# SBUF operands at multiples of 512 bytes, the router's rows by transposes, and matmuls of ones on an idle TensorE

## The chip, the cores and the metric

One core of one Trainium2 chip runs one launch of a hand-scheduled kernel. The metric is the device time of that launch in microseconds. All work is in fp32; products on TensorE are made of two halves of an fp32 number each (below).

## What is computed

The input is 512 tokens of width 1024. Two blocks follow one another.

```python
# first block
h = rglru_block(x, ...)                    # x @ w_in (1024 x 2560), gates, scan over time, @ w_out
x = layer_norm(ALPHA * x + h, ln_g[0, 0], ln_b[0, 0])
f = hier_moe(x, ...)                       # 4 groups x 8 experts, the best group's best 2 experts per token
x = layer_norm(ALPHA * x + f, ln_g[0, 1], ln_b[0, 1])
# second block, for each of two layers
x = x + 0.5 * swiglu(rmsnorm(x), w1_a, w3_a, w2_a)          # 1024 -> 2816 -> 1024
x = x + (gated sum of a Fourier, a convolution and a pooling branch) @ w_o
x = x + 0.5 * swiglu(rmsnorm(x), w1_b, w3_b, w2_b)
```

## The kernel before

**Split products.** Every large matrix product is three fp32r matmuls, of the high and low parts of both operands (`mm3`, lines 596 to 598: `L597` moves the low part of the data past high weights, and so on). ScalarE makes the high part of each 128x1024 block of weights (`w_hi`, `L1074`), VectorE the low part (`w_lo`, `L1699`). A ring of 5 to 14 raw buffers is filled by SyncE's queue, and the splits go into a ring of four. In a matmul one operand is loaded into the array (the stationary one, always 128 columns, 512 bytes per partition) and the other is moved past it: 512 columns in the recurrence, the mixers, the experts and the down products, 256 columns in the up products of the SwiGLUs, which are Strassen-like sums of quarters (`xf_hi`, `xf_lo`, and `e_hi`, `e_lo` for the combinations of weights).

**Stages in order of time** (us from the span's start): the recurrence to 222; layer norm, router and tables to 283; sixteen pairs of experts to 854; their combination to 892; then SwiGLU, mixers, SwiGLU for each of two layers to 2965; the rows of the result.

**The router's stage.** VectorE adds the residual to each 128-token tile of `x_tok` and normalises it (`L1804`, `L1789`, `L1812`). TensorE transposes it (`L602`), ScalarE applies gain and bias on the way to `x1T` (`L1167`), TensorE multiplies with the router's weights (`logits`, `L649`). Meanwhile GpSimd applies gain and bias to the rows in `x_tok` (`L1529`, `L1531`, with `gb` broadcast from HBM) and stores them to HBM (`x_rows`, `L1533`), from where the experts gather them. VectorE then chooses groups and experts in a chain of small steps (`L1844` to `L1866`), TensorE counts ranks (`L677`), VectorE computes places (to `L1916`), TensorE builds the table of token numbers with one-hot operands in fp32 (`L683`), VectorE turns it into indices, GpSimd issues the gathers (`L1542`), and TensorE transposes the gathered rows for the first pair (`x_turn`).

**Where operands lie.** Tensors stand one behind another in each partition, in the order of the `sb(...)` calls; a tensor that opens an `ExitStack` that was closed before begins again where that one began. In the program as built `raw` begins at byte 16,512. From the sizes it follows that, modulo 512 bytes, `raw`, `w_hi` and `w_lo` begin at 128; `x_tok`, `xc`, `x_hi`, `x_lo`, `g_hi`, `xg_hi`, `xf_hi`, `e_hi` and nearly all other matmul operands of the dense stages at 192; `xeT_hi`, `hT_hi`, `xe` and `hd` of the experts at 288. Slices of 128 fp32 columns keep these offsets.

**Queues.** SyncE loads the weights; ScalarE loads `gb` and the router's weights; GpSimd stores `x_rows`, gathers and scatters rows and loads the `sums` of the SwiGLUs. Each engine runs in program order and waits on semaphores.

Of the kernel before, what the change touches and what calls it, by code (L numbers as in the profile page):

```python
# [13 lines left out]
P = 128  # L14
# [58 lines left out]
C_ROW4 = C_SLOT + 2 * TT  # L73
# [136 lines left out]
def bank_table():  # L210
# [18 lines left out]
    for tt in range(TT):  # L229
        for half in range(2):  # L230
            use(("turn", tt, half), "x1t", 8 * tt + 4 * half + 4)
    use("lgt", "lgc", 2)
    use("rank", "lgc", 3)
# [75 lines left out]
xgh xgl xhi xhi2 xin xlo xlo0 xn xn2 xnv xr xtn yea yev yhi ylo yy zf zp zz""".split()  # L309


def build(nc, io):
    with ExitStack() as ctx:
# [12 lines left out]
        bank = [ctx.enter_context(nc.psum_tensor(f"bank{i}", [P, 512], F32)) for i in range(8)]  # L326
        raw = sb("raw", [P, NRAW, W])
# [4 lines left out]
        ones = sb("ones", [P, P])  # L332

        with ExitStack() as first:
# [15 lines left out]
            with ExitStack() as moe:  # L350
                raw_more = sb("raw_more", [P, NMORE, W], into=moe)
                gb = sb("gb", [P, 2, D], into=moe)
# [11 lines left out]
                oneh = sb("oneh", [P, 2 * TT, P], into=moe)  # L364
                blkh = sb("blkh", [P, 2 * TT, NBLK], into=moe)
                tabs = sb("tabs", [P, 4, NBLK], into=moe)
# [4 lines left out]
                cnt = sb("cnt", [P, 1], U32, moe)  # L371
                sil = sb("sil", [P, 2, FE], into=moe)
# [209 lines left out]
        def tensor_program(e):  # L582
# [21 lines left out]

            def in_tile(j):
# [40 lines left out]
            def logits(tt):  # L646
                e.wait_ge(s["x1t"], 8 * tt + 8)
                for k in range(DT):
                    f = e.matmul(bank[7][0:NG + NE, tt * P:(tt + 1) * P], wr[:, k, :], x1T[:, k, tt * P:(tt + 1) * P],  # L649
                                 start=k == 0, stop=k == DT - 1)  # L650
                f.then_inc(s["lgm"], 1)

            e.wait_ge(s["par"], 32)
            e.wait_ge(s["router"], 64)
# [15 lines left out]

            b = free_bank("rank")
# [53 lines left out]

            x_turn(0)
# [66 lines left out]
            def up_pair(i, j):  # L793
# [261 lines left out]
        def scalar_program(e):  # L1055
# [95 lines left out]
            e.dma_start(gb[:, 0, :], io["ln"][0:1, :].partition_broadcast(P)).then_inc(s["router"], 16)  # L1151
            e.dma_start(gb[:, 1, :], io["ln"][1:2, :].partition_broadcast(P)).then_inc(s["router"], 16)
# [3 lines left out]
            for tt in range(TT + 1):  # L1156
# [3 lines left out]
                if tt >= 1:  # L1160
                    a = tt - 1
                    for half in range(2):
                        e.wait_ge(s["turn"], 2 * a + half + 1)
                        b = bank_of(("turn", a, half))
                        for n in range(4):
                            k = 4 * half + n
                            e.activation(x1T[:, k, a * P:(a + 1) * P], b[:, n * P:(n + 1) * P], ACT.Identity,  # L1167
                                         scale=par("ln_g", k), bias=par("ln_b", k)).then_inc(s["x1t"], 1)

# [291 lines left out]
        def pool_program(e):  # L1461
# [62 lines left out]
            for tt in range(TT):  # L1524
                x = x_tok[:, tt, :]
                e.wait_ge(s["turn"], 2 * tt + 2)
                if tt == 0:
                    e.wait_ge(s["router"], 64)
                e.tensor_tensor(x, x, gb[:, 0, :], ALU.mult).then_inc(s["x1g"], 1)  # L1529
                e.wait_ge(s["x1g"], 2 * tt + 1)  # L1530
                e.tensor_tensor(x, x, gb[:, 1, :], ALU.add).then_inc(s["x1g"], 1)  # L1531
                e.wait_ge(s["x1g"], 2 * tt + 2)
                e.dma_start(x1_dram[tt * P:(tt + 1) * P, :], x).then_inc(s["x1d"], 16)  # L1533

# [11 lines left out]
            e.wait_ge(s["lgm"], TT)  # L1546
# [1001 lines left out]
```

## Time and profile before

| | |
|---|---|
| median of 3 runs | 2981.72 us (2980.78 to 2990.56) |
| the profiled execution, its own time | 2979.92 us |
| its span | 2978.1 us |
| mean granted TensorE clock | 0.979 |
| busy: TensorE matmuls, VectorE, ScalarE, GpSimd | 95%, 74%, 50%, 17% |
| HBM traffic | 175 GB/s over the span, 376 GB/s with the experts |

"Busy" of PE is the time in which at least one matmul is in flight; matmuls overlap, so at full occupation the pace is read from start to start, or from their number in a stretch. The granted clock is 1.00 where TensorE had its 2.4 GHz and 0.50 where it had 1.2 GHz.

### The profile page before, as it was taken

The numbers are of one execution on the slowest core, as the hardware profiler recorded it, in microseconds if no ns is written. First come the engines' busy times: TensorE is split into PE (matmuls) and PEld (weight loads), VectorE is DVE, ScalarE is ACT, GpSimd is POOL, SyncE is SP. The second block draws the span as 40 slices with busy tenths as digits, with TensorE's granted clock in tenths as the row PEclk, the third lists the DMA queues.
The fourth block names the chain that finished last, engine by engine and source line by source line (L and its number), as shares of the span: only waits on it lengthen the run. The fifth ranks groups of instructions, "written<-read, shape, count | busy, mean of one in ns | idle before, by whom it ended". The sixth has DMA issues, their size and how long they took to land.

```text
span 2978.1 us, 41904 instructions
## 1 busy us (share of the span) xinstructions
PE 2832.8 (95%) x16046; PEld 2448.9 (82%) x16046; DVE 2190.4 (74%) x2923; ACT 1498.7 (50%) x1998; POOL 491.8 (17%) x501
## 2 busy tenths in 40 slices
PE   8994999999957999999999999989999999989999
PEld 6673788888847999888888999889998888889997
DVE  6636999999978777766458777787676664687766
ACT  6833788888855444433235444454444332354443
POOL 3214011111012111110112111121111111131111
PEclk9996999999988999999999999999999999999999
DMA  5152999999955555232325655364643323256461
GB/s 216 50 181 77 343 378 374 372 373 375 376 188 138 160 156 163 94 102 93 96 95 139 173 142 169 108 169 132 184 133 101 101 92 101 92 138 181 133 184 59
DMA packets 169579, 516.25 MB, mean 173 GB/s; under 512 B 21536, under 2 KB 22048, under 8 KB 169120
## 3 DMA queue, kind: packets, MB, share of 16 engines
q1 hardware_dynamic: 129600, 422.38, 39.7%
q0 software_dynamic: 37568, 79.72, 12.7%
q10 hardware_dynamic: 2208, 11.43, 1.0%
q8 instruction: 130, 2.13, 0.3%
q14 instruction: 73, 0.60, 0.1%
HBM read 509.24 MB, written 12.58 MB: 175 GB/s over the span
## 4 chain that ended last, share of the span: by engine, by line
PE 82%; DVE 7%; issue 4%; ACT 2%; DMA 2%; POOL 2%; SPq 0%; DVEq 0%; ACTq 0%; POOLq 0%
PE bank L598 27%; PE bank L596 27%; PE bank L597 27%; DVE w_lo L1699 2%; ACT w_hi L1074 1%; PE bank L602 1%; DVE ft L2076 0%; DMA raw<-in_rec_in 0%; DMA raw<-in_w_b 0%; DMA raw<-in_w_a 0%; POOL mv L1506 0%; DVE st L1789 0%; POOL w_lo L1471 0%; DMA sums<-in_w_b 0%; DVE tmp L2132 0%
## 5 line engine op out<-in xcount | busy, mean ns | idle before, releaser
L1699 DVE TENSOR_TENSOR w_lo<-raw,w_hi 128x1024 fp32r<-128x1024 f32 (+3 forms) x481 | 593.2, 1251 | 287.8 <-ACT w_hi L1074 281.1
L1074 ACT ACTIVATE w_hi<-raw 128x1024 fp32r<-128x1024 f32 (+1 forms) x491 | 507.7, 1046 | 292.0 <-PE bank L598 284.8
L596 PE MATMUL bank<-xf_hi,w_lo 128*128 128x256 f32 x2112 | 592.3, 280 | 50.9 <-DVE xf_lo L2082 22.8
L598 PE MATMUL bank<-xf_hi,w_hi 128*128 128x256 f32 x2112 | 588.5, 279 | 0.0
L597 PE MATMUL bank<-xf_lo,w_hi 128*128 128x256 f32 x2112 | 588.4, 279 | 0.0
L596 PEld LDWEIGHTS bank<-xf_hi,w_lo 128*128 128x128 f32 x2112 | 401.1, 190 | 57.1 <-issue 24.4
L597 PEld LDWEIGHTS bank<-xf_lo,w_hi 128*128 128x128 f32 x2112 | 401.1, 190 | 2.4 <-issue 1.0
L598 PEld LDWEIGHTS bank<-xf_hi,w_hi 128*128 128x128 f32 x2112 | 400.7, 190 | 0.0
L1699 DVE TENSOR_TENSOR w_lo<-raw_more,w_hi 128x1024 fp32r<-128x1024 f32 x249 | 296.6, 1221 | 49.2 <-ACT w_hi L1074 46.5
L598 PE MATMUL bank<-g_hi,w_hi 128*128 128x512 f32 x832 | 327.5, 394 | 0.0
L597 PE MATMUL bank<-g_lo,w_hi 128*128 128x512 f32 x832 | 325.9, 392 | 0.0
L596 PE MATMUL bank<-g_hi,w_lo 128*128 128x512 f32 x832 | 323.6, 389 | 0.4 <-DVE g_lo L2119 0.4
L1074 ACT ACTIVATE w_hi<-raw_more 128x1024 fp32r<-128x1024 f32 x249 | 260.4, 1059 | 71.9 <-PE bank L598 71.6
L596 PE MATMUL bank<-xg_hi,w_lo 128*128 128x512 f32 x704 | 277.8, 395 | 0.2 <-issue 0.2
L598 PE MATMUL bank<-xg_hi,w_hi 128*128 128x512 f32 x704 | 277.8, 395 | 0.0
L597 PE MATMUL bank<-xg_lo,w_hi 128*128 128x512 f32 x704 | 277.2, 394 | 0.0
L596 PE MATMUL bank<-w_hi,xeT_lo 128*128 128x512 f32 x512 | 205.4, 401 | 1.5 <-DVE xeT_lo L1952 1.5
L598 PE MATMUL bank<-w_hi,xeT_hi 128*128 128x512 f32 x512 | 205.3, 401 | 0.0
L597 PE MATMUL bank<-w_lo,xeT_hi 128*128 128x512 f32 x512 | 203.3, 397 | 0.0
L597 PEld LDWEIGHTS bank<-g_lo,w_hi 128*128 128x128 f32 x832 | 156.2, 188 | 34.6
L596 PEld LDWEIGHTS bank<-g_hi,w_lo 128*128 128x128 f32 x832 | 156.2, 188 | 34.3 <-DVE g_lo L2119 1.2
L598 PEld LDWEIGHTS bank<-g_hi,w_hi 128*128 128x128 f32 x832 | 156.4, 188 | 31.7
(347 smaller groups left out, 5209.2 us busy)
## 6 DMA issues: line engine op xcount, KB each, us to landing
raw_more<-in_moe SPq DMA_DIRECT2D x249, 512.0 KB, 6.3
raw<-in_moe SPq DMA_DIRECT2D x135, 512.0 KB, 6.3
raw<-in_w_a SPq DMA_DIRECT2D x77, 512.0 KB, 5.0
raw<-in_w_b SPq DMA_DIRECT2D x76, 512.0 KB, 5.2
raw<-in_w_in SPq DMA_DIRECT2D x73, 512.0 KB, 3.6
sums<-in_w_a POOLq DMA_DIRECT2D x88, 256.0 KB, 4.7
sums<-in_w_b POOLq DMA_DIRECT2D x88, 256.0 KB, 4.8
raw<-in_w_a SPq DMA_DIRECT2D x68, 256.0 KB, 6.7
```

Source lines behind the costliest of these rows:

```text
L596: e.matmul(out, a_lo, b_hi, start=start, stop=False, skip_group_check=partial)
L597: e.matmul(out, a_hi, b_lo, start=False, stop=False, skip_group_check=partial)
L598: return e.matmul(out, a_hi, b_hi, start=False, stop=stop, skip_group_check=partial)
L602: last = e.transpose(out[:, n * P:(n + 1) * P], src(n), ident)
L1074: e.activation(split_of(k)[0], source_of(k), ACT.Copy).then_inc(s["hi"], 1)
L1699: e.tensor_tensor(lo, source_of(k), hi.bitcast(F32), ALU.subtract).then_inc(s["lo"], 1)
```

## The change

It has four parts. (1) Unused tensors (`pad_...`) move what stands behind them. In the program as built the weights, `x_hi`, `x_lo`, `xc`, `bd`, `g_hi`, `xg_hi`, `e_hi`, `sums`, `xe`, `hd`, `hT_hi` and `xeT_hi` now begin at 0 modulo 512; `xf_hi` and `xf_lo` begin at 64. (2) The rows of `x_tok` with gain and bias come from transposing `x1T` back on TensorE and copying them with ScalarE, which also issues the stores; GpSimd's eight multiplications and additions and `gb` are gone, and its `memset` of `xe` waits for the last of these transposes. The last half tile of `x1T` is made by VectorE. (3) The token numbers are split into a multiple of 32 and a rest, so that the table is made of bf16 operands. (4) `spin(n)` multiplies `ones` by `ones` n times into bank 7: 14 times at the start, 24 before the table, 16 behind it, and 10 before each of the last three k steps of the first product of the first SwiGLU pair.

```diff
+        sb("pad_raw", [P, 96])
         raw = sb("raw", [P, NRAW, W])
...
         ones = sb("ones", [P, P])
+        sb("pad_ones", [P, 104])
...
-                gb = sb("gb", [P, 2, D], into=moe)
...
-                oneh = sb("oneh", [P, 2 * TT, P], into=moe)
+                oneh = sb("oneh", [P, 2 * TT, P], BF16, moe)
+                numb = sb("numb", [P, 2, 2 * TT, NBLK], BF16, moe)
...
+                sb("pad_router", [P, 112], into=moe)
                 sil = sb("sil", [P, 2, FE], into=moe)
...
+            sb("pad_xf", [P, 16], into=ffn)
             xf_hi = sb("xf_hi", [P, KH, 7 * HALF], F32R, ffn)
             xf_lo = sb("xf_lo", [P, KH, 7 * HALF], F32R, ffn)
+            sb("pad_sums", [P, 112], into=ffn)
...
+            def spin(n):
+                for _ in range(n):
+                    e.matmul(bank[7][:, 0:P], ones[:, :], ones[:, :], start=True, stop=True)
...
+            e.wait_ge(s["cleared"], 2)
+            spin(14)
             for j in range(2 * RT):
...
+            for tt in range(TT):
+                for half in range(2):
+                    b = free_bank(("back", tt, half))
+                    transpose4(lambda n: x1T[:, 4 * half + n, tt * P:(tt + 1) * P], b).then_inc(s["turn"], 1)
             b = free_bank("rank")
...
+            spin(24)
             b = free_bank("table")
             e.wait_ge(s["idx"], 2)
             for n in range(2 * TT):
-                f = e.matmul(b[:, 0:NBLK], oneh[:, n, :], blkh[:, n, :], start=n == 0, stop=n == 2 * TT - 1)
+                e.matmul(b[:, 0:NBLK], oneh[:, n, :], numb[:, 0, n, :], start=n == 0, stop=False)
+                f = e.matmul(b[:, 0:NBLK], oneh[:, n, :], numb[:, 1, n, :], start=False, stop=n == 2 * TT - 1)
...
+            spin(16)
             x_turn(0)
...
                         for k in ks:
+                            if i == 0 and k >= 1:
+                                spin(10)
                             e.wait_ge(s["xgl"], ready + 4 * k + 1)
...
# ScalarE
+            for tt in range(TT):
+                for half in range(2):
+                    e.wait_ge(s["turn"], 2 * TT + 2 * tt + half + 1)
+                    e.activation(x_tok[:, tt, half * T:(half + 1) * T], bank_of(("back", tt, half))[:, :], ACT.Copy) \
+                        .then_inc(s["x1g"], 1)
+                e.wait_ge(s["x1g"], 2 * tt + 2)
+                e.dma_start(x1_dram[tt * P:(tt + 1) * P, :], x_tok[:, tt, :]).then_inc(s["x1d"], 16)
...
# GpSimd
-                e.tensor_tensor(x, x, gb[:, 0, :], ALU.mult).then_inc(s["x1g"], 1)
-                e.tensor_tensor(x, x, gb[:, 1, :], ALU.add).then_inc(s["x1g"], 1)
-                e.dma_start(x1_dram[tt * P:(tt + 1) * P, :], x).then_inc(s["x1d"], 16)
-            e.wait_ge(s["lgm"], TT)
+            e.wait_ge(s["turn"], 4 * TT)
             e.memset(xe[:, :, :], 0.0).then_inc(s["rows"], 1)
...
# VectorE
+            for n in range(4):
+                f = e.tensor_scalar(x1T[:, 4 + n, (TT - 1) * P:], bank_of(("turn", TT - 1, 1))[:, n * P:(n + 1) * P],
+                                    par("ln_g", 4 + n), par("ln_b", 4 + n), ALU.mult, ALU.add)
```

On TensorE, from the transposition of the logits to the first gathered rows, the program before has these rows (`consts` holds the identity):

```order
L649 MATMUL bank<-x1T,wr 36x128 x16
L667 MATMUL bank<-consts,lgT 128x36 x4
L677 MATMUL bank<-chosen,upper_b 128x32
...
L677 MATMUL bank<-chosen,ones_b 128x32 x4
L683 MATMUL bank<-blkh,oneh 128x31 x8
L602 MATMUL bank<-consts,xe 128x128 x8
```

and the changed program these:

```order
L669 MATMUL bank<-x1T,wr 36x128 x16
L687 MATMUL bank<-consts,lgT 128x36 x4
L612 MATMUL bank<-consts,x1T 128x128 x32
L702 MATMUL bank<-chosen,upper_b 128x32
...
L702 MATMUL bank<-chosen,ones_b 128x32 x4
L618 MATMUL bank<-ones 128x128 x24
L709 MATMUL bank<-numb,oneh 128x31
L710 MATMUL bank<-numb,oneh 128x31
...
L618 MATMUL bank<-ones 128x128 x16
L612 MATMUL bank<-consts,xe 128x128 x8
```

The 32 transposes back stand before the ranks, 24 products of ones stand before the table and 16 behind it. The table has 16 products of bf16 in place of 8 of fp32.

On GpSimd the program before has these rows between the recurrence and the first gathers (the first three repeat four times):

```order
L1529 TENSOR_TENSOR x_tok<-x_tok,gb 128x1024
L1531 TENSOR_TENSOR x_tok<-x_tok,gb 128x1024
L1533 DMA x_rows<-x_tok 128x1024
L1547 MEMSET xe 128x3072
L1542 DMA xe<-x_rows,gidx 128x1024 x2
```

and the changed program only these:

```order
L1572 MEMSET xe 128x3072
L1567 DMA xe<-x_rows,gidx 128x1024 x2
```

The eight wide operations and the four stores have left GpSimd; ScalarE has eight copies of 128x512 and the four stores in their place.

## Rows read from the trace of the kernel before

**Rows 1.** The page: the chain that ended last, by engine.

```profile
PE 82%; DVE 7%; issue 4%; ACT 2%; DMA 2%; POOL 2%; SPq 0%; DVEq 0%; ACTq 0%; POOLq 0%
```

**Rows 2.** Waits of TensorE in the whole span: us in total, times, longest.

```profile
PE bank L677 <- DVE chosen L1866: 10.1, 1, 10.1
PE bank L602 <- DMA xe<-x_rows,gidx: 6.7, 1, 6.7
```

**Rows 3.** Busy time by stretch: length, five engines, clock, DMA share, GB/s.

```profile
222.00:283.00 61.00, 23.34 (x147) 19.54 (x146) 46.05 (x107) 14.71 (x40) 28.95 (x18) 0.67 0.18 65
400.00:800.00 400.00, 400.00 (x1790) 323.71 (x1789) 373.79 (x355) 327.76 (x356) 40.24 (x21) 1.00 0.99 376
1345.00:1460.00 115.00, 115.00 (x494) 93.17 (x493) 67.96 (x87) 35.75 (x46) 12.54 (x15) 1.00 0.30 94
```

**Rows 4.** TensorE's groups by form: count, busy us, mean ns, idle before.

```profile
L598 PE MATMUL bank<-xf_hi,w_hi 128*128 128x256 f32 x2112 | 588.5, 279 | 0.0
L598 PE MATMUL bank<-g_hi,w_hi 128*128 128x512 f32 x832 | 327.5, 394 | 0.0
L598 PE MATMUL bank<-xg_hi,w_hi 128*128 128x512 f32 x704 | 277.8, 395 | 0.0
L598 PE MATMUL bank<-w_hi,xeT_hi 128*128 128x512 f32 x512 | 205.3, 401 | 0.0
L598 PE MATMUL bank<-xf_hi,e_hi 128*128 128x256 f32 x352 | 99.6, 283 | 0.0
```

**Rows 5.** TensorE in order of time, one SwiGLU pair: start us, duration.

```profile
1093.18 0.39 PE L596 MATMUL bank<-g_hi,w_lo 128*128 128x512 f32 x1
...
1104.17 0.28 PE L596 MATMUL bank<-xf_hi,w_lo 128*128 128x256 f32 x1
...
1117.77 0.28 PE L596 MATMUL bank<-xf_hi,e_lo 128*128 128x256 f32 x1
...
1120.65 0.28 PE L596 MATMUL bank<-xf_hi,w_lo 128*128 128x256 f32 x1
...
1123.37 0.39 PE L596 MATMUL bank<-g_hi,w_lo 128*128 128x512 f32 x1
```

**Rows 6.** All engines in order of time, router's stage.

```profile
227.92 0.81 DVE L1812 TENSOR_SCALAR x_tok<-x_tok,st 128x1024 f32<-128x1024 f32 x1
...
236.44 3.22 DVE L1812 TENSOR_SCALAR x_tok<-x_tok,st 128x1024 f32<-128x1024 f32 x1
...
244.93 2.90 ACT L1167 ACTIVATE x1T<-bank,params 128x128 f32<-128x128 f32 x8 [1.24 <-PE bank L602]
...
250.93 2.34 POOL L1531 TENSOR_TENSOR x_tok<-x_tok,gb 128x1024 f32<-128x1024 f32 x1
...
251.67 1.63 DVE L1845 TENSOR_TENSOR rt<-lg,sm 128x16 f32<-128x16 f32 x1
...
253.96 2.91 DVE L1849 TENSOR_SCALAR rt<-rt 128x16 f32<-128x16 f32 x1
254.16 2.68 POOL L1547 MEMSET xe<- 128x3072 f32 x1
...
272.24 3.59 PE L683 MATMUL bank<-blkh,oneh 128*128 128x31 f32 x16 [10.47 <-DVE blkh L1916]
```

**Rows 7.** The same view of TensorE: at the start, and where the experts begin.

```profile
8.33 0.76 PE L596 MATMUL bank<-x_hi,w_lo 128*128 128x512 f32 x1 [8.33 <-DVE x_lo L1727]
...
11.32 0.39 PE L597 MATMUL bank<-x_lo,w_hi 128*128 128x512 f32 x1
...
285.94 0.76 PE L596 MATMUL bank<-w_hi,xeT_lo 128*128 128x512 f32 x1 [1.50 <-DVE xeT_lo L1952]
...
291.13 0.40 PE L596 MATMUL bank<-w_hi,xeT_lo 128*128 128x512 f32 x1
```

**Rows 8.** Waits of TensorE from 860 to 975 us, round the first SwiGLU pair.

```profile
PE bank L596 <- DVE xf_lo L2082: 12.2, 2, 6.4
PE bank L596 <- ACT snap L1339: 2.7, 1, 2.7
```

More of the change, by code:

```diff
@@ L72 @@
 C_SLOT = C_EROW + TT * NE
-C_ROW4 = C_SLOT + 2 * TT
+C_REST = C_SLOT + 2 * TT
+C_ROW4 = C_REST + 2 * TT
 C_EDGE = C_ROW4 + 1
@@ L230, in bank_table @@
         for half in range(2):
-            use(("turn", tt, half), "x1t", 8 * tt + 4 * half + 4)
+            use(("turn", tt, half), *(("x1t", 8 * tt + 4 * half + 4) if (tt, half) != (TT - 1, 1) else ("x1v", 1)))
     use("lgt", "lgc", 2)
+    for tt in range(TT):
+        for half in range(2):
+            use(("back", tt, half), "x1g", 2 * tt + half + 1)
     use("rank", "lgc", 3)
@@ L646, in logits @@
             def logits(tt):
-                e.wait_ge(s["x1t"], 8 * tt + 8)
+                if tt < TT - 1:
+                    e.wait_ge(s["x1t"], 8 * tt + 8)
                 for k in range(DT):
+                    if tt == TT - 1 and k % 4 == 0:
+                        e.wait_ge(*((s["x1v"], 1) if k else (s["x1t"], 8 * tt + 4)))
                     f = e.matmul(bank[7][0:NG + NE, tt * P:(tt + 1) * P], wr[:, k, :], x1T[:, k, tt * P:(tt + 1) * P],
@@ L653, in tensor_program @@
             e.wait_ge(s["par"], 32)
-            e.wait_ge(s["router"], 64)
+            e.wait_ge(s["router"], 32)
             for tt in range(TT):
@@ L1161, in scalar_program @@
                     a = tt - 1
-                    for half in range(2):
+                    for half in range(2 if a < TT - 1 else 1):
                         e.wait_ge(s["turn"], 2 * a + half + 1)
@@ L1168, in scalar_program @@
                                          scale=par("ln_g", k), bias=par("ln_b", k)).then_inc(s["x1t"], 1)
+            for tt in range(TT):
+                for half in range(2):
+                    e.wait_ge(s["turn"], 2 * TT + 2 * tt + half + 1)
[3 more added lines that the diff above has]
+                e.dma_start(x1_dram[tt * P:(tt + 1) * P, :], x_tok[:, tt, :]).then_inc(s["x1d"], 16)
             e.wait_ge(s["gat"], 1)
@@ L1522, in pool_program @@
                 weights(2 * RT + k)
[L1524 to L1528, printed above, removed]
-                e.tensor_tensor(x, x, gb[:, 0, :], ALU.mult).then_inc(s["x1g"], 1)
-                e.wait_ge(s["x1g"], 2 * tt + 1)
-                e.tensor_tensor(x, x, gb[:, 1, :], ALU.add).then_inc(s["x1g"], 1)
-                e.wait_ge(s["x1g"], 2 * tt + 2)
-                e.dma_start(x1_dram[tt * P:(tt + 1) * P, :], x).then_inc(s["x1d"], 16)
             def gather(n):
@@ L1816, in vector_program @@
             e.tensor_copy(upper_b[:, :], upper)
+            e.wait_ge(s["turn"], 2 * TT)
+            for n in range(4):
+                f = e.tensor_scalar(x1T[:, 4 + n, (TT - 1) * P:], bank_of(("turn", TT - 1, 1))[:, n * P:(n + 1) * P],
+                                    par("ln_g", 4 + n), par("ln_b", 4 + n), ALU.mult, ALU.add)
+            f.then_inc(s["x1v"], 1)
             e.wait_ge(s["lgm"], TT)
-            e.wait_ge(s["router"], 64)
+            e.wait_ge(s["router"], 32)
             e.tensor_scalar(lgT[:, :], bank[7][0:NG + NE, :], br[:, :], None, ALU.add).then_inc(s["lgc"], 1)
@@ L2506, in lay_out @@
         for tt in range(TT):
-            c[:, C_SLOT + k * TT + tt] = k * T + tt * P + np.arange(P) + 1
+            number = k * T + tt * P + np.arange(P) + 1
+            c[:, C_SLOT + k * TT + tt] = number - number % 32
+            c[:, C_REST + k * TT + tt] = number % 32
     c[:, C_ROW4] = 4 * np.arange(P)
```

12 lines of the change are left out of this document (6 added, 6 removed).

## Prediction

> **What bounds the kernel now.** I read the page first. Matmuls are in flight for 95% of the span, as the table of the profile says, and the chain that ended last runs through TensorE for 82% of it [rows 1]. So I asked next, stretch by stretch, whether TensorE waits or is only slow. With the experts (400 to 800 us) it is busy for all of 400 us, and no release of another engine stands in front of it; VectorE is busy for 373.8 of the 400 us, and the DMA engines for 0.99 of the time at 376 GB/s [rows 3]. In the mixers TensorE is again at 100%, with VectorE at 68 of 115 us [rows 3]. The waits that are left lie in the router's stage, where TensorE works 23 of 61 us at a mean clock of 0.67 [rows 3], waits 10.47 us for the table's operands [rows 6] and 6.7 us for the gathered rows [rows 2], and round the first SwiGLU pair [rows 8].
>
> So two quantities decide: how long the router's chain takes, and at what pace matmuls follow each other where nothing waits. The pace is to be read from start to start, as the durations of rows 4 overlap. One SwiGLU pair gives three paces in a row [rows 5]. The 120 matmuls of 256 columns with a block of `w` as the stationary operand take from 1104.17 to 1117.77, 113.3 ns each. The 24 with `e` take from 1117.77 to 1120.65, 120.0 ns each, and the 24 with `w` behind them 2.72 us, 113.3 ns each. The columns, the clock and the moving tensor (`xf`, at 192 modulo 512) are the same; what differs is the stationary operand, which lies at 128 (64 bytes apart from `xf`, modulo 128) or at 192 (0 apart). The 48 matmuls of 512 columns before them take from 1093.18 to 1104.17, 229.0 ns each; from 1345 to 1460 us of the mixers 494 take 115 us, 233 ns each [rows 3], with the same offsets and without a wait. At half the clock 12 matmuls of 512 columns take from 285.94 to 291.13, 432 ns each [rows 7], about one clock cycle a column; at the full clock the same cycle count would be some 213 ns. So at the full clock something takes 7 to 9%, and it depends on where the operands lie, and for 512 columns also on something that changes during the run.
>
> With the experts, a turn of one pair is 144 matmuls of 512 columns and 12 transposes; 1790 matmuls in 400 us [rows 3] are 34.9 us a turn. With some 0.11 us for a transpose that leaves 233 ns for one of 512 columns, with 160 bytes between the offsets.
>
> **The router's stage, part by part.**
>
> *GpSimd's work goes.* VectorE normalises a tile in 0.81 us where GpSimd is idle, and takes 3.22 us for the third tile while GpSimd multiplies `x_tok` by `gb`; the four take 0.81, 1.60, 3.22 and 2.65 us, 5.0 us more than four times 0.81. A step on 16 elements takes 1.63 us while GpSimd ends `L1531`, and one 2.91 us while its `memset` runs [rows 6]; their neighbours take 0.17. The Trainium skill says the same as a rule (SBUF — State Buffer, on its two separate sides): VectorE's two-port operations and GpSimd share a port pair under an exclusive lock. The trace agrees: the step at 251.67 ends where the GpSimd operation that began at 250.93 ends. Of the 5.0 us I count 3.8, since TensorE's transposes of the last tile also queue behind the logits of the second; of the two small steps 1.5 and 2.7. The `memset` stays, but it waits for the transposes back and so falls on two-operand steps of the choice. Together 8.0 us.
>
> *Half of the last tile on VectorE.* ScalarE takes 2.90 us for eight pieces [rows 6]; with four of them on VectorE at the same time 1.2 us go.
>
> *The table.* 16 passes in fp32 take 3.59 us [rows 6]. Sixteen in bf16 with 31 columns are bounded from above by the same passes (no gain) and from below by nothing (3.6). I take 3.0, since the loading of 128 fp32 columns sets the pace of the present ones, at half clock. One more VectorE operation like the one before it costs 0.4.
>
> *What is added.* 32 transposes of 128 columns, priced from above like a pass of the table in rows 6 (0.22 us at half clock), are 7 us on TensorE. They stand in its wait of 10.1 us for the chosen experts [rows 2], ahead of the ranks. Of that wait the 4.2 us of blocked small steps go, so 6 us are free, and up to 1 us may be paid. ScalarE's eight copies and four stores follow beside them and end long before the gather asks for the rows, some 20 us later. ScalarE has nothing else there, and its exponentials are wanted only behind the gather's indices. 24 products of ones are 48 passes, 10.2 us at half clock; the wait that covers them is 10.47 us [rows 6]. The 16 behind the table, 6.8 us at most, lie in the wait of 6.7 us for the gather [rows 2] and the index steps of 2.4 us ahead of it. SyncE's queue is not touched; ScalarE's and GpSimd's queues exchange four stores. Sum: 8.0 + 1.2 + 3.0 - 0.4 = 11.8 us less.
>
> *The clock.* If ones keep TensorE at the full clock, the 12 matmuls of rows 7 take 233 instead of 432 ns, 2.4 us less, and the eight transposes ahead of them 0.7. At the start, the matmuls from 8.33 to 11.2 us run at half clock (7 of them) [rows 7]; 14 products of ones ahead may save 1.4 us, as nothing but TensorE is late there. Sum 4.5. In the first SwiGLU pair TensorE also works at half clock, but it then waits 2.7 us for ScalarE's `snap` and 12.2 us for `xf_lo` before that [rows 8]: VectorE's and ScalarE's splitting of the rows sets the time. A faster clock there ends in a longer wait, so I count nothing; should a spin of 20 passes (4.3 us) outlast a wait, the wait of 2.7 us behind it covers it.
>
> The router and the clock give 16.3 us. The unknown ends are 9 and 20.
>
> **The operands' places.** Matmuls by pace: 832 x 3 of `g`; 704 x 3 of `xg` and, by the loops, 344 x 3 more of the recurrence and the mixers; 768 x 3 of the experts (512 x 3 with `xeT`, half as many with `hT`); 2112 x 3 of `xf` with `w`; 352 x 3 with `e` [rows 4].
>
> After the change `xf` lies 64 bytes past `w`, as before, and now also past `e`. If the distance is what counts, the 1056 matmuls with `e` take 113.3 ns: 7.1 us less. If it is not, nothing.
>
> All matmuls of 512 columns come from distances of 64 (dense) or 160 (experts) to 0. No row shows 512 columns at distance 0 or at multiples of 512. The bounds: from above 240 ns, twice the 120.0 of `e`, the only pair at distance 0. From below the cycle count, 213 ns. The value that I take is 226.7 ns, twice 113.3: the pace of a stream of 256 columns where the two reads agree best, which the 512-column ones nearly reach in their faster stretches (229.0). It gives 2496 x 2.3 = 5.7 us for `g`; 3144 x 4.3 = 13.5 for the other dense ones (between 229 and 233 ns now, 231 on the mean); 2304 x 6.6 = 15.2 with the experts. Sum 34.4. There the DMA engines and VectorE have room for a few per cent: the stage is 2.9% faster, VectorE goes from 93.4% to 96%.
>
> I choose the better half of the bounds because the 229 and 233 of the same operands show that the loss comes and goes with how two streams meet, so equal places for all of them can remove it, while the row of `e` speaks only for 256 columns at 192. This is the weakest step.
>
> The Trainium skill (TensorE: Matmul & The Clock Gate, on the back-to-back issue gap) gives N/2.4 + 2.5 ns, 215.8 for 512 and 109.2 for 256 columns; no row here reaches it. Its SBUF page says that loading the next weights takes nothing from the moving operand; rows 5 differ, 120.0 against 113.3 ns, and by that page the places would be worth nothing at all.
>
> **Sum.** 16.3 + 7.1 + 34.4 = 57.8 us off the span of 2978.1, so 2920.3; the profiled run's own time is 1.8 longer than its span, the median of the runs again 1.8 longer: **2924 us**.
>
> **Rivals.**
>
> *The places do nothing for 512 columns.* For it: 229 and 233 ns occur at one and the same distance. Against it: `e`. Then 16.3 + 7.1 = 23: 2958 us. A variant in which distance 0 costs what 64 costs in its slower stretches (233.3 throughout) loses 2496 x 4.3 + 3144 x 2.3 = 18 us and gives 2976, no change that can be told.
>
> *The matmuls reach the bare stream.* For it: at half clock they do. With 216 ns for 512 columns (2496 x 13 = 32 us, 3144 x 15 = 47) and 109 for 256 (6336 x 4.3 = 27, 1056 x 11 = 12). With the experts VectorE becomes the bound: it is at 93.4%, so no more than 6.6% of 554 us, 36 us, can go. That is 154 + 16: 2812 us.
>
> *Slower: distance 0 is bad.* If a stationary operand at distance 0 costs 512 columns what `e` costs 256, they go to 240 ns: 2496 x 11 = 27, 3144 x 9 = 28, 2304 x 6.7 = 15, 71 us in all against 16 + 7: 3029 us. For it: rows 5, the only direct evidence on distance 0. It decides from 234 ns on, where it outweighs the router's 23 us.
>
> *Ones delay what they fill.* 24 products have 10.2 us in a wait of 10.5 that itself becomes later or earlier; if the clock stays low and the ranks come a microsecond late, TensorE reaches the table a microsecond late. Within the 9 us end above.
>
> **How the numbers follow.** Chances: 226.7 ns or near it 0.36; nothing for 512 columns 0.22; bare stream 0.18; 233.3 ns 0.10; slower 0.14. The range 2838 to 2985 leaves out the last and the lowest part of the bare stream. The likeliest case by itself spans 2905 to 2945. A measurement of this kernel tells 0.3% (9 us) from no change. Faster by more: 0.36 + 0.22 + 0.18 = 0.76; same 0.10; slower 0.14.
>
> **What the changed kernel's profile would show.** The starts of 24 matmuls with `e` 2.72 us apart in place of 2.88; 48 of `g` in 10.9 us or less; a mixers' stretch at one pace; more than 1830 matmuls in 400 us of the experts. `L1812`'s successor at 0.8 us four times, no small step above 0.3 us, the table under 1 us, the first matmul of the experts some 12 to 13 us earlier and at 0.23 us. In the first SwiGLU pair more clock and the same end. The prediction is wrong if the paces of 512 columns stand at 229 and 233 still, or at 240, or below 220.

## The result and the profile after

The changed kernel takes 2968.19 us, the median of seven runs (2962.95 to 2973.13), against 2985.49 for the kernel before in the same comparison (2980.78 to 2990.56). The ratio is 0.9945, with an interval of 0.9932 to 0.9959: faster by 16 us. I had forecast 2924 from 2982, 57 us less. The sign was right and the size was not. The profiled execution took 2965.37 us with a span of 2963.5, against 2979.92 and 2978.1 before, so there are 14.6 us in the two traces to be accounted for.

In the page, the chain that ended last still runs through TensorE, as in [rows 1]:

```profile
PE 81%; DVE 8%; issue 5%; ACT 3%; DMA 2%; POOL 2%; SPq 0%; DVEq 0%; ACTq 0%; POOLq 0%
```

The busy time by stretch (columns as in [rows 3]) shows the router's stage shorter and the rest denser. In 400 us of the experts 1832 matmuls start where 1790 did, and in 115 us of the mixers 508 where 494 did:

```profile
222.00:270.00 48.00, 33.53 (x254) 30.42 (x253) 35.27 (x111) 16.71 (x43) 6.79 (x5) 0.86 0.18 66
400.00:800.00 400.00, 400.00 (x1832) 331.86 (x1831) 381.66 (x365) 335.40 (x364) 42.26 (x22) 1.00 1.00 385
1345.00:1460.00 115.00, 115.00 (x508) 95.16 (x508) 65.58 (x78) 37.01 (x48) 12.90 (x10) 1.00 0.29 94
```

Where nothing waits in the mixers, the matmuls of 512 columns now stand at one pace, 226.7 to 227 ns; the kernel before had 233.3 in some stretches and 229 in others, with the same operands. The same SwiGLU pair as in [rows 5], TensorE in order of time (start, duration):

```profile
1069.87 0.40 PE L606 MATMUL bank<-g_hi,w_lo 128*128 128x512 f32 x1
...
1080.79 0.28 PE L606 MATMUL bank<-xf_hi,w_lo 128*128 128x256 f32 x1
...
1094.92 0.28 PE L606 MATMUL bank<-xf_hi,e_lo 128*128 128x256 f32 x1
...
1097.75 0.28 PE L606 MATMUL bank<-xf_hi,w_lo 128*128 128x256 f32 x1
...
1100.58 0.40 PE L606 MATMUL bank<-g_hi,w_lo 128*128 128x512 f32 x1
```

This is where the forecast broke. The 48 matmuls of `g` take 10.92 us, 227.5 ns each (229.0 before). But the 120 of `w` and `xf` take 14.13 us, 117.8 ns each, where they took 113.3, although `xf` still lies 64 bytes past `w`. The 24 with `e` take 2.83 us, 117.9 ns (120.0 before), and the 24 behind them 2.83, which were 2.72. One such round of the loop, 48 of `g`, 120 of `xf` with `w`, 24 with `e` and 24 with `w` again, is called a turn below; it takes 30.71 us in place of 30.19.

The router's stage, all engines in order of time, answers to [rows 6]:

```profile
231.03 0.81 DVE L1837 TENSOR_SCALAR x_tok<-x_tok,st 128x1024 f32<-128x1024 f32 x1
...
245.03 3.71 PE L612 MATMUL bank<-consts,x1T 128*128 128x128 f32 x32
245.69 0.17 DVE L1875 TENSOR_TENSOR rt<-lg,sm 128x16 f32<-128x16 f32 x1
...
246.51 0.17 DVE L1879 TENSOR_SCALAR rt<-rt 128x16 f32<-128x16 f32 x1
...
251.40 7.23 PE L618 MATMUL bank<-ones 128*128 128x128 f32 x48
...
262.35 0.18 PE L709 MATMUL bank<-numb,oneh 128*128 128x31 bf16 x1 [3.71 <-DVE numb L1949]
...
262.78 5.21 PE L618 MATMUL bank<-ones 128*128 128x128 f32 x32
```

All four normalisations take 0.81 us, no small step is above 0.3 us, the table takes 0.43 us (262.35 to 262.78), and its operands come at 262.35 in place of 272.24. The ones before it end 3.7 us ahead of its operands.

A wait stands among those of TensorE which the kernel before does not have. Its place is the entry of the second layer's mixers. Behind it the clock is granted at 0.50 for 6.8 us. The fences give the view of waits, the view in order of time, and the busy time by stretch:

```profile
PE bank L606 <- DVE xT L2160: 4.6, 1, 4.6
```

```profile
2262.53 0.39 PE L608 MATMUL bank<-g_hi,w_hi 128*128 128x512 f32 x1
2267.53 0.77 PE L606 MATMUL bank<-xg_hi,w_lo 128*128 128x512 f32 x1 [4.61 <-DVE xT L2160]
...
2271.93 0.63 PE L607 MATMUL bank<-xg_lo,w_hi 128*128 128x512 f32 x1
```

```profile
2265.90:2272.70 6.80, 5.17 (x12) 4.13 (x13) 4.06 (x5) 3.47 (x4) 1.40 (x3) 0.50 0.34 96
```

To see where the time went I cut both spans at the same matmuls, by their starts in the trace. A is up to the first gathered rows, B the experts (up to the last transposes of `hd`), C what is left of them, the combination and the first SwiGLU pair's first products, D the rest of the four SwiGLUs up to the last `g` matmul, E all between and behind them, the mixers above all. Microseconds, from the profiled executions of both kernels and of six of the experiments:

| kernel | A | B | C | D | E | span |
|---|---|---|---|---|---|---|
| before | 282.5 | 555.5 | 82.2 | 1308.8 | 749.1 | 2978.1 |
| after | 269.8 | 540.7 | 83.9 | 1322.7 | 746.4 | 2963.5 |
| e1, places alone | 279.6 | 541.5 | 83.9 | 1325.2 | 740.4 | 2970.6 |
| e5, after with the old ring | 269.8 | 537.6 | 84.2 | 1326.2 | 742.6 | 2960.4 |
| e9, before with g moved | 279.4 | 555.6 | 82.2 | 1320.1 | 747.7 | 2985.0 |
| e10, g and e moved back | 272.1 | 539.1 | 84.4 | 1307.6 | 739.1 | 2942.3 |
| e11, e 64 past xf | 271.7 | 537.5 | 84.1 | 1302.8 | 739.3 | 2935.4 |
| e12, router alone | 270.8 | 554.0 | 84.5 | 1312.0 | 750.1 | 2971.4 |

After against before: A -12.7, B -14.8, C +1.7, D +13.9, E -2.7. A and B gave nearly what was forecast, and half of it is lost again in D.

Inside D the matmuls can be counted by kind, from start to start, in the two traces. The 6048 of `xf` with `w` take 714.2 us where they took 692.5, 21.7 more. The 1056 with `e` take 129.4 for 133.7, 4.3 less. The 2112 of `g`, without the wait of 4.6 us, take 3.4 less.

### The profile page after: what moved, and what is told of

Same layout as the page of the kernel before. It is cut to its first block, busy times and chain, and to the rows that moved or that the text cites. A ratio compares the mean times of both kernels' runs of the same rounds, so it can differ in the third digit from the quotient of the medians.

```text
span 2963.5 us, 42302 instructions
## 1 busy us (share of the span) xinstructions
PE 2851.8 (96%) x16246; PEld 2496.5 (84%) x16246; DVE 2178.6 (74%) x2928; ACT 1501.5 (51%) x2002; POOL 469.9 (16%) x489
## 4 chain that ended last, share of the span: by engine, by line
PE 81%; DVE 8%; issue 5%; ACT 3%; DMA 2%; POOL 2%; SPq 0%; DVEq 0%; ACTq 0%; POOLq 0%
PE bank L606 27%; PE bank L608 26%; PE bank L607 26%; DVE w_lo L1724 2%; ACT w_hi L1104 1%; PE bank L612 1%; DVE xT L2160 1%; DVE ft L2109 1%; DMA raw<-in_w_b 0%; DMA raw<-in_rec_in 0%; ACT sq L1311 0%; DMA raw<-in_w_a 0%; POOL mv L1542 0%; POOL w_lo L1507 0%; DVE ft L2119 0%
## 5 line engine op out<-in xcount | busy, mean ns | idle before, releaser
L606 PE MATMUL bank<-xf_hi,w_lo 128*128 128x256 f32 x2112 | 598.9, 284 | 40.4 <-ACT snap L1375 18.0
L606 PE MATMUL bank<-xg_hi,w_lo 128*128 128x512 f32 x704 | 275.9, 392 | 4.6 <-DVE xT L2160 4.6
```

The source lines that it names most:

```text
L606: e.matmul(out, a_lo, b_hi, start=start, stop=False, skip_group_check=partial)
```

## The experiments

Behind each median below stand four to eleven runs, beside runs of the kernel before on the same chip; e4 and e8 ran once.

**e1: the places alone.** The kernel before with only the unused tensors:

```diff
+        sb("pad_raw", [P, 96])
+        sb("pad_ones", [P, 112])
+                sb("pad_router", [P, 104], into=moe)
+            sb("pad_xf", [P, 16], into=ffn)
+            sb("pad_sums", [P, 112], into=ffn)
```

> The kernel before with the padding alone, so that each of TensorE's operands lies where the change puts it (modulo 512: weights, g, xg, e, experts at 0, xf at 64); router, table and queues as before, no products of ones. Theory A (the places set the pace, whatever runs around them): the experts' stage is 14 to 15 us shorter than before, each SwiGLU turn is 30.7 us in place of 30.2, the mixers some 3 us shorter each, so that the whole is 0 to 6 us faster than before. Theory B (the pace of the changed kernel comes from when things happen, its router and its ones, and not from the places): paces as before, the experts at 34.9 us a turn and the whole within 3 us of before. By my prediction the places alone are worth 41 us.

Measured: 2970.27 us, ratio 0.9955 (0.9941 to 0.9968), 13 us faster. The experts' stage is 14.0 us shorter than before and D 16.4 us longer. The paces thus come with the places and not with the router or the ones. The whole is more than theory A gave it, because E falls by 8.7 us, and A by 2.9. The 2.9 are no effect of the places that the prediction names. In the kernel before the `memset` holds up one small step for 2.91 us [rows 6]; here it begins beside a step with two operands and holds up none:

```profile
254.85 2.68 POOL L1552 MEMSET xe<- 128x3072 f32 x1
254.89 0.29 DVE L1861 TENSOR_TENSOR rt<-rt,sm 128x128 f32<-128x128 f32 x1
```

The wait for the chosen experts is 8.4 us in place of 10.1. e9, which has the router of before as well, shows the same (A 279.4). So with one and the same router the experts begin at 279.4 to 282.5 us, and a gain of 12.7 us at A contains some 3 us of this.

**e2: no ones.** `for _ in range(n)` in `spin` became `range(0)`; this takes out all 84 products (14, 24, 16 and 3 x 10; the expectation counts the last kind wrongly).

> The changed kernel without any product of ones (all 14, 24, 16 and 4 x 3 x 10 of them). By my prediction's terms: 1.4 us later at the start, 3.1 us later where the experts begin, nothing in the first SwiGLU pair, 4.5 us slower than the changed kernel. Rival: the ones also cost something where they stand (the wait for ScalarE and the splitting in the first pair is overrun), then it is less than 2 us slower, or faster. If the 118 ns of the 256-column matmuls were brought about by the ones, these would run at 113 ns here and the kernel would be 20 us faster than the changed one.

Measured: 2970.63 us, ratio 0.9957 (0.9944 to 0.9971), against 0.9945 for the changed kernel: the intervals overlap. In the traces the experts begin 1.6 us later than with ones and C is 0.7 us longer. The ratios differ by 3.6 us and the spans of the two traces by 5.3, which neither confirms nor refutes the 4.5 us that I gave the ones; only the 1.6 and 0.7 us lie where they stand. The 118 ns do not come from them: D stays at 1323.3.

**e3: everything 128 bytes further.**

```diff
-        sb("pad_raw", [P, 96])
+        sb("pad_raw", [P, 128])
```

> The changed kernel with the first padding 32 elements longer: every operand lies 128 bytes further, so all distances between operands are the same and w stands at 128 and xf at 192 modulo 512, the places of the kernel before in which 256 columns took 113.3 ns. Theory A1 (the distance decides): no change, 118 ns, within 3 us of the changed kernel. Theory A2 (the place itself decides, modulo 256 or 512): 256 columns at 113.3 ns and SwiGLU turns of 30.2 us, 18 to 23 us faster than the changed kernel, 2946 us. Theory B (a lock of the streams that comes and goes): some turns at 30.2 and some at 30.7.

Measured: 2966.82 us, ratio 0.994 (0.9925 to 0.9954), as the changed kernel; D is 1324.0. `w` at 128 and `xf` at 192 are the very places of before, and still the pace is 118 ns. It is not the place itself.

**e4: the pace of each pair of places.** Nothing of the kernel is left but matmuls. In the names, `sthi64x` is a stationary block 64 bytes past that of `sthi0x`, modulo 512, and `mv...` the moving operand likewise. Each stretch is 96 matmuls of one pair of places. The core of it:

```diff
+            for lap in range(3):
+                for p in (MIXED if lap == 1 else STRETCHES):
+                    f = stretch(*p)
```

> A measurement by itself: it leaves the reference's computation out altogether. TensorE runs 48 stretches of 96 fp32r matmuls (stationary block at 0, 64, 128 or 192, moving operand at 0, 32, 64, 128, 192 or 320 modulo 512; 256 and 512 columns), three terms of a hi and a lo part in the order of the kernels, in three laps: in one order with nothing else running, in another order, and in the first order again with VectorE and the loads of weights running. Theory A1 (distance decides): 256 columns take one time for each distance modulo 128, 113 or 118 ns at 64, 120 at 0. Theory A2 (place): the row for stationary 128 differs from that for 0 at the same distance. Theory B (lock): one pair of places has different paces in the first and the second lap. Theory C (other engines' traffic makes the loss): laps one and two at 107 to 109 and 213 to 216 ns for all places, the third slower.

TensorE in order of time. First 256 columns, starts of the stretches for a moving operand 64, 128, 192 and 320 bytes past the stationary one; then one of the second lap; then 512 columns at 0, 64 and 192:

```profile
48.92 0.28 PE L397 MATMUL bank<-mvhi64x,stlo0x 128*128 128x256 f32 x1
...
60.24 0.28 PE L397 MATMUL bank<-mvhi128x,stlo0x 128*128 128x256 f32 x1
...
71.63 0.28 PE L397 MATMUL bank<-mvhi192x,stlo0x 128*128 128x256 f32 x1
...
82.52 0.28 PE L397 MATMUL bank<-mvhi320x,stlo0x 128*128 128x256 f32 x1
...
1342.96 0.28 PE L397 MATMUL bank<-mvhi192x,stlo0x 128*128 128x256 f32 x1
...
1354.26 0.28 PE L397 MATMUL bank<-mvhi128x,stlo192x 128*128 128x256 f32 x1
...
297.48 0.40 PE L397 MATMUL bank<-mvhi0x,stlo0x 128*128 128x512 f32 x1
...
319.29 0.40 PE L397 MATMUL bank<-mvhi32x,stlo0x 128*128 128x512 f32 x1
...
341.70 0.40 PE L397 MATMUL bank<-mvhi64x,stlo0x 128*128 128x512 f32 x1
...
363.68 0.39 PE L397 MATMUL bank<-mvhi128x,stlo0x 128*128 128x512 f32 x1
...
385.98 0.40 PE L397 MATMUL bank<-mvhi192x,stlo0x 128*128 128x512 f32 x1
...
408.39 0.39 PE L397 MATMUL bank<-mvhi320x,stlo0x 128*128 128x512 f32 x1
```

96 matmuls of 256 columns take 11.31 us at 64 bytes past (117.8 ns) and 10.89 at 192 (113.5), but the same pair takes 11.30 in the second lap, behind another stretch. With 512 columns they take 21.81 us at equal places (227.2 ns), 21.98 at 64 (229.0) and 22.41 at 192 (233.4). Over all 48 pairs the paces sort by the difference modulo 256; at some differences there are two. The paces (the differences 32, 96, 160 and 224 stand on one pair of places each, in three laps):

| moving operand past the stationary, modulo 256 | 0 | 32 | 64 | 96 | 128 | 160 | 192 | 224 |
|---|---|---|---|---|---|---|---|---|
| 256 columns, ns | 119.9 | 116.7 or 117.8 | 117.8 | 119.9 | 118.6 | 117.3 | 113.5 or 117.8 | 118.3 |
| 512 columns, ns | 227.1 | 233.4 | 229.0 | 233.3 | 232.3 or 233.3 | 234.2 | 233.3 | 233.3 |

Theory C is out. The third lap repeats the first beside VectorE at full occupation and loads at 373 GB/s, and its stretches start where those of the first did, to 0.1 ns a matmul. The same 100 us of both laps, by stretch:

```profile
67.00:167.00 100.00, 100.00 (x853) 100.00 (x852) 0.00 (x0) 0.00 (x0) 1.00 0.00 1
1676.43:1776.43 100.00, 100.00 (x853) 100.00 (x852) 100.00 (x167) 0.00 (x0) 1.00 0.98 373
```

Theory A1, the distance alone, fails for 256 columns: at 192 two paces are possible. For 512 columns it holds in these laps but for a difference of 1 ns at 128; in the kernel before, though, 512 columns at 64 run at 229 in some stretches and at 233 in others [rows 3, 5]. What was left to find was what chooses between them, since 64 past gives 117.8 here and gave 113.3 in the kernel before.

**e5: the ring of banks.** The tiles behind the router take PSUM banks in a ring of seven. The eight new transposes use eight, so every later tile has the next bank.

```diff
             use(("back", tt, half), "x1g", 2 * tt + half + 1)
+    turn[0] += 6
```

> The changed kernel, with six turns of the ring of seven PSUM banks skipped behind the eight transposes back, so that every tile behind them has the bank that it had before the change. In the changed kernel's trace TensorE waits 4.6 us at 2262.5 for the bank of the second layer's first mixer tile, which is the one that the SwiGLU's seventh sum leaves last, and its clock is halved for 6.8 us from 2265.9 on. Theory D (the eight new uses moved the ring by one, and that costs 4.6 + 2 us): the wait is gone, the second layer's entry takes 12.1 us from the last g matmul to the end of the first mixer tiles as before, in place of 18.9, and the kernel is 6 to 7 us faster than the changed one, 2961. Rival: the wait only moves to the next bank, no change.

Measured: 2962.25 us, ratio 0.9938 (0.9924 to 0.9951). The wait of 4.6 us is gone:

```profile
2265.29 0.47 PE L607 MATMUL bank<-xg_hi,w_lo 128*128 128x512 f32 x1 [0.26 <-DVE xT L2161]
```

The stretch from the last `g` matmul of the third SwiGLU to the fourth takes 350.9 us in place of 356.7, and the clock stays full there. Between this kernel and the changed one the whole times are not told apart: the ratios differ by 2 us, less than their intervals. Between e7 and e6, which differ in the same line and ran side by side, the intervals do not overlap.

**e6 and e7: `xf` at 192 with `w` and `e` at 0**, 64 bytes before them modulo 256, without and with the edit of e5:

```diff
-            sb("pad_xf", [P, 16], into=ffn)
+            sb("pad_xf", [P, 48], into=ffn)
-            sb("pad_sums", [P, 112], into=ffn)
+            sb("pad_sums", [P, 80], into=ffn)
```

> The changed kernel with xf 128 bytes further, at 192 modulo 512 with w and e at 0: the moving operand stands 64 bytes ahead of the stationary one, modulo 256. In the measurement of places by itself this was the only distance at which 256 columns took 113.5 ns in most stretches (117.8 at 64 bytes past, 119.9 at equal places). Theory A3 (the distance modulo 256 sets the pace, 64 ahead is best for 256 columns): SwiGLU turns of 30.1 us in place of 30.7, 7392 matmuls at 113.5 in place of 118 are 33 us; 2936 us. Theory B (two paces are possible at this distance too, as one of three stretches showed, and what runs ahead decides which): some or all stretches at 118, between 2936 and 2968 us.

> Both of these edits together: xf at 192 modulo 512 and the ring of banks as it was. If they are independent, the sum of the two gains, 2929 us by theories A3 and D; this is the candidate that should beat both kernels.

Measured: e6 2967.15 us, ratio 0.995 (0.9937 to 0.9964); e7 2957.38, ratio 0.9919 (0.9905 to 0.9932). The better distance brought nothing: all turns of both are at 30.7 us. My theory A3 fell. The ring is worth 9 us between the two by the ratios; in their traces the stretch named under e5 is 5.0 us shorter with it (5.8 from the changed kernel to e5).

**e8: the SwiGLU's turn by itself** (48 matmuls of `g`, 120 of `xf` with `w`, 24 with `e`, 24 with `w`), two turns of each of 18 layouts:

```diff
+            for lap in range(2):
+                for p in (MIXED if lap else CASES):
+                    turn(*p)
+                    f = turn(*p)
```

> A measurement by itself, which leaves the reference's computation out: TensorE runs the SwiGLU's turn (48 matmuls of g and w with 512 columns, 120 of xf and w with 256, 24 of xf and e, 24 of xf and w), twice for each of 18 layouts (w at 0; xf at 64, 128 or 192; e at xf's place, 64 before it or 192 before it modulo 256; g at 0 or 64), in two orders. Theory B (two paces are possible for xf 64 past w, and what ran ahead decides): with e at xf's place, as before the change, the stretches of xf and w behind it run at 113.3 ns, with e 64 before it, as after the change, at 117.8. Theory A1 (distance alone): 117.8 in both. At 192 both theories expect 113.5, or, where a stretch falls into the other pace, 117.8.

TensorE in order of time. `xhi64x` lies 64 past `w` in all of these; `ghi0x` at `w`'s place, `ghi64x` 64 past it; `elo64x` at `xf`'s place, `elo128x` 64 past `xf`:

```profile
62.40 0.28 PE L388 MATMUL bank<-xhi64x,w_lo 128*128 128x256 f32 x1
...
76.53 0.28 PE L388 MATMUL bank<-xhi64x,elo64x 128*128 128x256 f32 x1
...
79.40 0.28 PE L388 MATMUL bank<-xhi64x,w_lo 128*128 128x256 f32 x1
...
82.12 0.39 PE L388 MATMUL bank<-ghi64x,w_lo 128*128 128x512 f32 x1
...
123.30 0.28 PE L388 MATMUL bank<-xhi64x,w_lo 128*128 128x256 f32 x1
...
136.90 0.28 PE L388 MATMUL bank<-xhi64x,elo64x 128*128 128x256 f32 x1
...
1628.13 0.28 PE L388 MATMUL bank<-xhi64x,w_lo 128*128 128x256 f32 x1
...
1642.27 0.28 PE L388 MATMUL bank<-xhi64x,elo128x 128*128 128x256 f32 x1
...
1658.92 0.28 PE L388 MATMUL bank<-xhi64x,w_lo 128*128 128x256 f32 x1
...
1672.52 0.28 PE L388 MATMUL bank<-xhi64x,elo128x 128*128 128x256 f32 x1
```

Behind `g` at `w`'s place the 120 matmuls take 14.13 us (117.8 ns). The 24 behind `e` at `xf`'s place, with the same two operands, take 2.72 (113.3). Behind `g` 64 past `w` the 120 take 13.60 (113.3 ns). The last four rows are the same layout twice in a row, 14.14 and then 13.60 us. So `xf` 64 past `w` has two paces that last for as long as the stream does. What runs ahead decides. `g` at `w`'s place is followed by the slow pace in all of 12 turns, `g` 64 past `w` by the fast one in 9 of 12; the other three begin behind a turn of another layout or follow a turn that was slow, and what decides there is not found. `e` at `xf`'s place is followed by the fast one in all of 8 turns, whatever stood ahead of it. With `e` 64 bytes before `xf`, as in the changed kernel, the slow pace went through in all 6 turns that had it. That is the change: it put `g` where the slow pace begins, and `e` where it is not left again. With `e` 64 bytes past `xf` the fast pace follows in 7 of 8 turns. The paces of `xf` 128 past `w` move with `g` too: 120.0 ns behind `g` at `w`'s place, 118.6 behind `g` 64 past it. It also explains e6: in the turns of e8 with `xf` 64 before `w` the 120 matmuls ran at 117.8 ns in all 24 turns, whichever place `g` had.

**e9: the kernel before with `g` alone at `w`'s place.** This tests that in the kernel, from the other side.

```diff
+        sb("pad_g", [P, 112])
         g_hi = sb("g_hi", [P, 8, T], F32R)
...
+            sb("pad_xf", [P, 16], into=ffn)
...
+            sb("pad_xg", [P, 16], into=mix)
```

> The kernel before with one thing changed: g lies at w's place (128 modulo 512) in place of 64 past it; xf stays 64 past w, e at xf's place, everything else where it was. Theory B (256 columns with xf 64 past w have two lasting paces, and g at w's place throws them into the slow one): in each SwiGLU turn the 120 matmuls of w and xf behind g go from 113.3 to 117.8 ns, the 24 behind e stay at 113.3, the turn goes from 30.2 to 30.6 us, and the kernel is 12 to 18 us SLOWER, although g itself goes from 229 to 227 ns. Theory A (each pair's distance alone sets its pace, as my prediction had it): 4 to 6 us faster.

Measured: 2992.28 us, ratio 1.0046 (1.0033 to 1.0059), 14 us slower by the ratio. One turn:

```profile
1092.12 0.39 PE L599 MATMUL bank<-g_hi,w_lo 128*128 128x512 f32 x1
...
1103.02 0.28 PE L599 MATMUL bank<-xf_hi,w_lo 128*128 128x256 f32 x1
...
1117.16 0.28 PE L599 MATMUL bank<-xf_hi,e_lo 128*128 128x256 f32 x1
...
1122.75 0.39 PE L599 MATMUL bank<-g_hi,w_lo 128*128 128x512 f32 x1
```

`g` itself is a little faster, 10.90 us for 48, and the 120 behind it take 14.14 us. D grows by 11.3 us.

**e10 and e11: the changed kernel with the ring of e5 and `g` 64 past `w` again**, with `e` at `xf`'s place (e10) or 64 bytes past `xf` (e11; the padding of 16 in front of `sums` stands only there).

```diff
+        sb("pad_g", [P, 16])
         g_hi = sb("g_hi", [P, 8, T], F32R)
...
-            sb("pad_xf", [P, 16], into=ffn)
-            sb("pad_sums", [P, 112], into=ffn)
+            sb("pad_sums", [P, 16], into=ffn)
...
+            sb("pad_xg", [P, 112], into=mix)
```

> The changed kernel with the ring of banks as it was, and with g 64 bytes past w and e at xf's place again, as before the change; all other operands as the change puts them (xf 64 past w; xg, pc, experts at w's place). Theory B: the lock is in the fast pace again, turns of 30.2 us: 6336 matmuls at 113.3 in place of 117.8 are 28 us, e goes from 117.8 to 120 (2), g from 227 to 229 (5): 21 us faster than with the ring alone, 2941 us. Theory A: 7 us slower than with the ring alone, 2969.

> As the one before, but with e 64 bytes ahead of xf (e at 128, xf at 64, modulo 256). In the turns measured by themselves this pair ran at 113.4 ns and brought the stretches behind it back to the fast pace when they had fallen out of it, so it should hold in all four SwiGLUs: turns of 30.0 us, another 7 us less, 2934 us. If the recovery does not happen in the kernel, as e10. Theory A: at least 4 us slower than with the ring alone.

Measured: e10 2943.37 us, ratio 0.9875 (0.9861 to 0.989); e11 2938.98 us, ratio 0.9867 (0.9852 to 0.9881). Against e5 that is 19 and 21 us by the ratios, for a few unused bytes. In e10 all turns are at 30.2 us, in e11 nearly all at 30.0. The turn in e11:

```profile
1065.93 0.39 PE L608 MATMUL bank<-g_hi,w_lo 128*128 128x512 f32 x1
...
1076.91 0.28 PE L608 MATMUL bank<-xf_hi,w_lo 128*128 128x256 f32 x1
...
1090.51 0.28 PE L608 MATMUL bank<-xf_hi,e_lo 128*128 128x256 f32 x1
...
1095.95 0.39 PE L608 MATMUL bank<-g_hi,w_lo 128*128 128x512 f32 x1
```

It takes 30.02 us: `g` 10.98, `w` and `xf` 13.60, `e` and the rest 5.44, all 48 of these at 113.3 ns. e11 beats the kernel before by 41 us in the medians, and the changed kernel by 23 us by the ratios.

**e12: the router and the ones alone.** The changed kernel with the operands at the places of before and the ring of e5.

```diff
-        sb("pad_raw", [P, 96])
...
-        sb("pad_ones", [P, 104])
+        sb("pad_ones", [P, 120])
...
-                sb("pad_router", [P, 112], into=moe)
+                sb("pad_router", [P, 8], into=moe)
...
-            sb("pad_xf", [P, 16], into=ffn)
-            sb("pad_sums", [P, 112], into=ffn)
```

> The changed kernel with all operands at the places of before (modulo 512) and the ring of banks as it was: what is left is the router's part and the ones. By my prediction 16.3 us faster than before, with bounds of 9 and 20; by the stages of the changed kernel's trace 12.7 us at the start of the experts, of which nothing is lost later if the ring is right: 2969 to 2972 us.

Measured: 2973.28 us, ratio 0.9975 (0.9966 to 0.9984), 7 us faster (5 to 10), where the prediction has 16.3 and no less than 9. The experts begin 11.7 us earlier than in the trace of before, but only 8.6 earlier than in e9, and C is 2.3 us longer and D 3.2. The turns are at 30.2 us with some at 30.7, which the kernel before also has, at other times. So in this layout some stretches fall into the slow pace and others not; what picks them is not shown.

## Why the prediction was right and where it failed

**GpSimd's work: the mechanism right, the agreement of the sum luck.** The logits' additions start 6.0 us earlier (243.87 for 249.85 us), the ranks 10.2 us earlier, the table's operands 9.9 and the table's end another 3 us; 0.9 us of all that is from ahead of the router. In sum 11.8 us are gained between the end of the recurrence and the gathered rows, and 11.8 was forecast. Its terms are seen in the trace: wide operations at 0.81 us, small steps at 0.17, a table of 0.43 us, and 0.3 us for the additional step. But that the sum agrees to 0.1 us is luck. The trace of before has the 2.7 us of the `memset` on a small step, which e1 and e9 do not have; against them the changed kernel's rows come 9.7 us earlier and not 12.7. And e12 gets 7 us for the router and the ones together, where 16.3 were forecast.

**The clock: half of it.** I gave the ones 4.5 us. The recurrence ends 0.9 us earlier instead of 1.4; in e5, the same program up to there, it ends 2.6 us earlier, since its clock stays full at 146 us where the changed kernel's is granted at 0.50 for 3.4 us. So a term of this size is not safe in one trace. Where the experts begin, 8 matmuls still run at half the clock where 12 did [rows 7]:

```profile
272.63 0.77 PE L606 MATMUL bank<-w_hi,xeT_lo 128*128 128x512 f32 x1 [1.73 <-DVE xeT_lo L1985]
...
276.08 0.39 PE L608 MATMUL bank<-w_hi,xeT_hi 128*128 128x512 f32 x1
```

The 16 ones end at 268.0, the wait for the rows and then 1.7 us for `xeT_lo` follow, and the clock is low from 272.5 to 275.9. Together with 0.65 us in front of them that makes 1.5 for 3.1. In the first SwiGLU pair nothing was gained, as forecast.

**512 columns: right.** The value chosen was 226.7 ns. Where the places are equal 227.1 is measured in e4, 227.5 for `g`, and 34.1 us a turn with the experts. B fell by 14.8 us, of which 1.5 are the clock's, so 13.3 are left for the 15.2 forecast (2304 x 6.6; from the 233 ns that the prediction reads it would be 6.3 a matmul, 14.5 us). The mixers and what lies round them gave 9.5 us without the ring's loss, for 13.5 forecast, of which 3.1 (720 x 4.3 ns) stood on the recurrence, where no such gain is seen. The three rivals with other paces for 512 columns are out, the slower one with it: distance 0 is the best for 512 columns, and for 256, at 119.9 ns, it is with 96 the slowest. No pair reaches the bare stream. The Trainium skill's rule (TensorE: Matmul & The Clock Gate, on the back-to-back issue gap) gives, as an estimate, 215.8 and 109.2 ns. No stretch of these runs is below 226.7 and 113.3, so the measurement decides against it for these operands.

**256 columns: the step that failed.** It was the sentence "After the change `xf` lies 64 bytes past `w`, as before", from which I counted nothing for the 6336 matmuls of `xf` and `w`, and 7.1 us for those with `e`. I had taken the pace as a property of the pair. It is one of the pair and of what ran ahead: 6336 x 4.5 ns would be 28.5 us, less the slow turns that the kernel before has too, and 21.7 us more are measured in D. The term for `e` gave 4.3 us of its 7.1, since `e` too came to 117.9 ns and not to 113.3, and `g` 3.4 in D. D rose by 13.9 us, and by my terms (5.7 for `g`, 7.1 for `e`) it should have fallen by 12.8. That is 26.7 of the 43 us between forecast and traces. e8 shows the mechanism by itself, e9 makes the kernel before 14 us slower with it, e10 takes it out of the changed kernel. The clue stood in the trace of before: 229 and 233 ns at one distance. I had used it to argue for equal places, and never asked whether 113.3 had a second value as well. The first turns of the second SwiGLU take 30.7 us there.

**What was missing: the ring.** I went through every queue that the 32 transposes are moved past, but not through the numbering of the banks that they take. Eight uses in a ring of seven moved each later tile by one bank, and one of them then waited 4.6 us and lost 2.2 us more to the clock (12 matmuls at 427 ns, in part). That is 6.8 us where it happens; e5 wins 5.8 of them back in that stretch, but its E falls by 3.8 only, so of the whole the ring may explain less. The remaining 9.7 us are the dense stages (4.0), the experts (1.9), the clock (2.1) and C (1.7). Why C takes some 84 us (86.6 in e3) in place of 82 in all kernels but the one before and e9 stays open.

## What to carry to other kernels

Where matmuls follow each other without a wait, read the pace from start to start for each kind, over the whole run, and look for a second value before you call it a property of the operands: here a change to one operand's place moved the pace of matmuls that it does not touch. Measure turns in the order of the kernel, not single pairs, since e4 alone led to e6, which was worth nothing. When an edit takes a few more turns of a ring of buffers, count them modulo the ring's length, and look at who gets which buffer hundreds of microseconds later.

## What the runs showed of the hardware

- With fp32r operands, at the full clock, no stretch was faster than 113.3 ns for 256 and 226.7 ns for 512 columns, with nothing else running on the core. At half the clock a column takes one cycle (427 ns for 512); at the full one 17 for 16 at best.
- The pace depends on the difference between the addresses of moving and stationary operand modulo 256 bytes (e4). 512 columns run best at 0 (227.1); 256 columns run slowest there at 0 and 96 (119.9).
- At a difference of 64, and of 192, 256 columns have two paces, 113.3 to 113.5 and 117.8 ns (e4, e8). A change from one to the other was seen only where another kind of matmul came between. 512 columns at 64 have two as well, 229 and 233 ns, in the kernel before. Why, no run here shows.
- A GpSimd operation on 128x1024 and the `memset` hold up steps of VectorE: a step on 16 elements took 1.63 and 2.91 us in place of 0.17. Beside the same `memset` in e1 two-operand steps kept their 0.29 us.
- VectorE at full occupation and loads at 373 GB/s do not change the pace of a matmul by 0.1 ns.
